# A two-block hybrid layer in fp32: index keys joined with head weights, scores dealt out between products, a split moved among selection rounds, and an output in token halves

## What is computed

```python
h = rms_norm(x, norm_g) * (1 + scale) + shift
ssm_u, ssm_z, q, k, v, attn_z, q_idx, k_idx, w_idx = split(h @ w_in)   # k_idx 64 wide, w_idx 8
z = gelu(s5(ssm_u)); z = z * sigmoid(z @ w_glu + b_glu)                # y_ssm = z * silu(ssm_z)
rel = einsum('bqhd,bsd->bqhs', q_idx, k_idx)                           # 8 heads
score = einsum('bqh,bqhs->bqs', w_idx * 8 ** -0.5, relu(rel))          # causal
_, sel = top_k(score, 128)
...
merged = sum(gates * projected)                                        # three branches
x = x + rmsnorm(merged @ w_out2, norm_mix_post)
h = rmsnorm(x, norm_ffn_pre)
x = x + rmsnorm((silu(h @ w_gate) * (h @ w_up)) @ w_down, norm_ffn_post)
```

## Time and profile before

| | |
|---|---|
| median of 3 runs | 1620.63 us (1618.85 to 1621.23) |
| the profiled execution's own time | 1621.4 us |
| its span, first to last instruction | 1619.6 us |
| mean granted TensorE clock | 0.972 of 2.4 GHz |
| PE busy | 1520.5 us (94%) |
| DVE busy | 884.5 us (55%) |
| ACT busy | 592.2 us (37%) |
| DMA | 152.24 MB, mean 94 GB/s |

### The profile page before, as it was taken

The page is one execution under the profiler, slowest core; times in us unless marked ns, Lnnn a source line. Parts: engine busy times, 40 slices in busy tenths (PEclk is TensorE's granted clock), DMA queues, the critical chain, the costliest instruction groups (busy, mean ns, idle before and its releaser), DMA issues.

```text
span 1619.6 us, 19347 instructions
## 1 busy us (share of the span) xinstructions
PE 1520.5 (94%) x7862; PEld 1209.2 (75%) x7862; DVE 884.5 (55%) x1383; ACT 592.2 (37%) x875; POOL 23.7 (1%) x36
## 2 busy tenths in 40 slices
PE   4899994989999999999999999999998999999995
PEld 2576783666888788777788887888876888888884
DVE  6878858687554766243635534553347644444233
ACT  3333423466333655133425533332334322222220
POOL 0010110000000000000000000000000000000000
PEclk9898997999999999999999999999998999999998
DMA  8422152204322121121222221222331323222221
GB/s 324 158 90 69 67 127 95 78 27 156 130 104 79 53 78 54 52 79 59 98 89 101 79 79 52 79 88 95 104 130 52 105 104 104 91 92 98 98 91 52
DMA packets 23271, 152.24 MB, mean 94 GB/s; under 512 B 3328, under 2 KB 3888, under 8 KB 6912
## 3 DMA queue, kind: packets, MB, share of 16 engines
q1 hardware_dynamic: 20720, 137.43, 24.0%
q0 software_dynamic: 2464, 13.59, 3.0%
HBM read 144.55 MB, written 7.88 MB: 94 GB/s over the span
## 4 chain that ended last, share of the span: by engine, by line
PE 87%; DVE 8%; ACT 2%; issue 1%; DMA 1%; SPq 0%; DVEq 0%; ACTq 0%
PE bank L530 85%; DVE score L1992 1%; DVE small L1991 1%; DMA xr<-xT 1%; PE bank L936 1%; DVE rstd L1784 1%; DVE w_lo L1764 0%; ACT w_hi L1154 0%; DVE sgb L1728 0%; DVE down L2579 0%; DVE tval L1950 0%; DVE y_lo L1779 0%; PE bank L868 0%; DVE score L2021 0%; DVE h_lo L1779 0%
## 5 line engine op out<-in xcount | busy, mean ns | idle before, releaser
L530 PE MATMUL bank<-h_hi,w_hi 128*128 128x512 f32 x1112 | 446.5, 402 | 12.0 <-DVE h_lo L2516 7.8
L530 PE MATMUL bank<-h_hi,w_lo 128*128 128x512 f32 x1128 | 443.6, 393 | 0.0
L530 PE MATMUL bank<-h_lo,w_hi 128*128 128x512 f32 x1112 | 437.3, 393 | 0.0
L1764 DVE TENSOR_TENSOR w_lo<-w_raw,w_hi 128x2048 fp32r<-128x2048 f32 (+2 forms) x109 | 245.5, 2253 | 269.4 <-ACT w_hi L1154 267.6
L1154 ACT CAST w_hi<-w_raw 128x2048 fp32r<-128x2048 f32 (+2 forms) x110 | 206.3, 1875 | 178.1 <-PE bank L530 175.5
L530 PEld LDWEIGHTS bank<-h_hi,w_hi 128*128 128x128 f32 x1112 | 210.8, 190 | 67.8 <-issue 21.0
L530 PEld LDWEIGHTS bank<-h_hi,w_lo 128*128 128x128 f32 x1128 | 213.5, 189 | 46.4
L530 PEld LDWEIGHTS bank<-h_lo,w_hi 128*128 128x128 f32 x1112 | 210.9, 190 | 45.0 <-issue 1.7
L530 PE MATMUL bank<-y_hi,w_hi 128*128 128x512 f32 x272 | 112.7, 414 | 22.1 <-DVE y_lo L1779 22.1
L530 PE MATMUL bank<-y_hi,w_lo 128*128 128x512 f32 x272 | 106.9, 393 | 0.0
L530 PE MATMUL bank<-y_lo,w_hi 128*128 128x512 f32 x272 | 106.7, 392 | 0.0
(11 more groups left out here) (365 smaller groups left out, 1830.8 us busy)
## 6 DMA issues: line engine op xcount, KB each, us to landing
w_raw<-wstream SPq DMA_DIRECT2D x120, 1024.0 KB, 4.8
xr<-xT SPq DMA_DIRECT2D x2, 2048.0 KB, 10.2
w_raw<-wstream SPq DMA_DIRECT2D x4, 768.0 KB, 4.2
bias_rows<-bias_table POOLq DMA_DIRECT2D x1, 2560.0 KB, 13.0
bias<-bias_rows POOLq DMA_DIRECT2D x1, 2048.0 KB, 12.4
x_saved<-xr POOLq DMA_DIRECT2D x1, 2048.0 KB, 9.6
xr<-x_saved POOLq DMA_DIRECT2D x1, 2048.0 KB, 9.0
outT<-down SPq DMA_DIRECT2D x8, 256.0 KB, 2.0
```

The costliest lines, as they stand in the source:

```text
L530: return pe.matmul(out, lhsT, rhs, start=start, stop=stop)
L1764: dve.tensor_tensor(w_low_of(s)[:, 0:kt, :], w_raw[:, i % RAW_SLOTS, 0:kt, :], hi_of(s)[:, 0:kt, :].bitcast(f32), ALU.subtract).then_inc(w ...
```

## The change

Five edits come together. (1) The tile of the index keys holds 64 key columns and 8 head-weight columns side by side, one product makes 72 rows, ACT copies the keys and scales the head weights, and a POOL DMA copies the keys to the other 64 partitions. (2) Two relevance matmuls stand after every second step of the q products, a fourth bank is used, and DVE's rotations, low splits and two selection rounds are cut into pieces with one piece behind a score. (3) `toep` is cleared by ACT. (4) 14 of the 23 selection rounds stand ahead of the low split of the first glu tile, 9 behind. Six of the low parts of `merged` are made before the last two merge steps. (5) The last group of `ffn_down` runs over all three tiles for tokens 0 to 255 and then for 256 to 511, the third tile has its high part in `w_wide`, and statistics, root, reciprocal, last operations and DMAs are done for each half. Names of semaphores and some plain renamings are left out.

```diff
-    ("k_idx", [("w_in", 0, KT, [(3584, 64), (3584, 64), (3648, 8)])]),
+    ("k_idx", [("w_in", 0, KT, [(3584, 64), (3648, 8)])]),
...
+        WIDE = (G["ffn_up"][1].s, G["ffn_down"][3].s + 2)
+        HALF = SEQ // 2
         def hi_of(s):
-            return w_wide[:, :, :] if s == G["ffn_up"][1].s else w_hi[:, s % 2]
+            return w_wide[:, :, :] if s in WIDE else w_hi[:, s % 2]
...
+        REL_BANKS = (5, 6, 7, 3)
+        ROTATE = {8: (1, 0), 9: (1, 1), 10: (1, 2), 11: (2, 0), 12: (2, 1), 13: (2, 2), 14: (3, 0), 15: (3, 1),
+                  16: (3, 2), 17: (4, 0), 18: (4, 1), 19: (4, 2), 24: (5, 0), 25: (5, 1)}
...
+            pool.wait_ge(ki_copied, 1)
+            pool.dma_start(ki[64:128, :], ki[0:64, :]).then_inc(ki_doubled, 16)
...
-            pool.memset(toep[:, :, :], 0.0).then_inc(toep_zero, 1)
...
-                mm(bank[b[0]][:, :], wh[:, k, 0:P], h_hi[:, k, :], k == 0, False)
-                mm(bank[b[0]][:, :], wh[:, k, 0:P], h_lo[:, k, :], False, False)
-                ins = mm(bank[b[0]][:, :], wl[:, k, 0:P], h_hi[:, k, :], False, k == KT - 1)
-            ins.then_inc(group_done, 1)
-            for k in range(KT):
-                out = bank[b[1]][0:HEADS, :]
-                mm(out, wh[:, k, P:P + HEADS], h_hi[:, k, :], k == 0, False)
-                mm(out, wh[:, k, P:P + HEADS], h_lo[:, k, :], False, False)
-                ins = mm(out, wl[:, k, P:P + HEADS], h_hi[:, k, :], False, k == KT - 1)
-            ins.then_inc(group_done, 1)
+                out = bank[b[0]][0:64 + HEADS, :]
+                mm(out, wh[:, k, 0:64 + HEADS], h_hi[:, k, :], k == 0, False)
+                mm(out, wh[:, k, 0:64 + HEADS], h_lo[:, k, :], False, False)
+                ins = mm(out, wl[:, k, 0:64 + HEADS], h_hi[:, k, :], False, k == KT - 1)
+            ins.then_inc(group_done, 2)
...
-                    if i >= 3:
-                        pe.wait_ge(relu_ready, i - 2)
-                    mm(bank[5 + i % 3][:, 0:P * (qt + 1)], qi[hp, h // 2, qt * P:qt * P + P],
+                    if i >= 4:
+                        pe.wait_ge(relu_ready, i - 3)
+                    mm(bank[REL_BANKS[i % 4]][:, 0:P * (qt + 1)], qi[hp, h // 2, qt * P:qt * P + P],
...
+            pe.wait_ge(ki_doubled, 16)
             relevance(0, 3)
+            pe.wait_ge(wi_ready, 1)
+            relevance(3, 4)
             for w, gr in enumerate(G["q"]):
                 for half in range(2):
                     n = 2 * w + half
-                    gemm_half(gr, half, "fm", h_hi, h_lo)
-                    relevance(3 + 8 * n, min(11 + 8 * n, 32))
-                    if n:
-                        query_stats(n - 1)
+                    for k in range(KT):
+                        gemm_unit(gr, half, k, h_hi, h_lo)
+                        if k % 2:
+                            i = 8 * n + k + 3
+                            relevance(i, min(i + 2, 32))
+                        if n and k == 5:
+                            query_stats(n - 1)
...
+            for gr in G["ffn_down"][:3]:
                 gemm_long(gr, f_hi, f_lo, AT["f"])
-            presummed("post2")
-            last_stats("post2")
+            def end_stats(t):
+                c, s0 = end_cols(t), SQ0["post2"] + 6 + 2 * t
+                out = stat_bank("post2")[:, c]
+                pe.wait_ge(root_ready, ROOT["post2"] + t)
+                pe.wait_ge(presum_ready, PRESUM.index("post2") + 1)
+                mm(out, ones[:, :], rstd[:, c], True, False)
+                for half in range(2):
+                    pe.wait_ge(sq_ready, s0 + half + 1)
+                    mm(out, ones[:, :], sqb[:, half, c], False, half == 1).then_inc(sq_used, 1)
+            gr = G["ffn_down"][3]
+            for t in range(2):
+                for half in range(2):
+                    pe.wait_ge(bank_free[end_bank(t, half)], end_uses(t, half))
+                for j, kt in enumerate(gr.kts):
+                    wh, wl = hi_of(gr.s + j), w_low_of(gr.s + j)
+                    pe.wait_ge(w_low, gr.s + j + 1)
+                    for half in range(2):
+                        c = slice(half * P, half * P + P)
+                        out = bank[end_bank(t, half)][:, 0:HALF]
+                        for k in range(kt):
+                            a = KT * j + k
+                            pe.wait_ge(act_low, AT["f"] + a + 1)
+                            mm(out, wh[:, k, c], f_hi[:, a, end_cols(t)], a == 0, False)
+                            mm(out, wh[:, k, c], f_lo[:, a, end_cols(t)], False, False)
+                            ins = mm(out, wl[:, k, c], f_hi[:, a, end_cols(t)], False, a == FT - 1)
+                        if j == 2:
+                            ins.then_inc(end_done, 1)
+                        if t and j == 0 and half == 0:
+                            end_stats(0)
+            end_stats(1)
...
+            bk = pbanks(gr)
+            act.wait_ge(group_done, 2 * gr.g + 1)
+            act.copy(ki[0:64, :], bank[bk[0]][0:64, :]).then_inc(ki_copied, 1)
+            act.activation(sqb[64:64 + HEADS, 0, :], bank[bk[0]][64:64 + HEADS, :], ACT.Copy,
+                           scale=float(HEADS) ** -0.5).then_inc(wi_row, 1)
+            act.wait_ge(ki_copied, 1)
+            act.wait_ge(wi_row, 1)
+            for half in range(2):
+                act.nop().then_inc(bank_free[bk[half]], 1)
...
-            relus(0, 3)
+            relus(0, 4)
             for n in range(4):
                 if n == 2:
                     ahead(G["q"][1])
-                relus(3 + 8 * n, min(11 + 8 * n, 32))
+                relus(4 + 8 * n, min(12 + 8 * n, 32))
                 head_chunk("q", n, q32)
+            act.activation(toep[:, :, :], ones[:, 0:1, None].to_broadcast([P, GROUPS, P]), ACT.Copy, scale=0.0)\
+               .then_inc(toep_zero, 1)
...
+            for t in range(2):
+                c, s0 = end_cols(t), SQ0["post2"] + 6 + 2 * t
+                for half in range(2):
+                    act.wait_ge(end_done, 2 * t + half + 1)
+                    act.wait_ge(sq_used, s0 + half - 1)
+                    act.activation(sqb[:, half, c], bank[end_bank(t, half)][:, 0:HALF], ACT.Square).then_inc(sq_ready, 1)
+                act.wait_ge(sq_used, s0 + 2)
+                act.wait_ge(rstd_ready, ROOT["post2"] + t)
+                act.activation(root[:, c], stat_bank("post2")[:, c], ACT.Sqrt, bias=eps[:, 0:1],
+                               scale=1.0 / D).then_inc(root_ready, 1)
...
+                if i // 4 in (1, 5):
+                    split_low_part(6 + i // 16, i % 4)
+                if i in ROTATE:
+                    rotations(*ROTATE[i])
+                if i in (26, 27):
+                    select_keys(1)
...
+            select_keys(14)
             split_low(G["glu"][0].s)
-            select_keys(23)
+            select_keys(9)
...
+            def merged_low(m):
+                dve.nop().then_inc(act_val, 1)
+                low(AT["merged"] + m, h_lo[:, m, :], h_hi[:, m, :], merged[:, m, :])
             for j in range(16):
                 if j % 2 == 0:
                     ahead(G["merge1"][j // 2])
+                if j == 14:
+                    for m in range(6):
+                        merged_low(m)
                 merge_part(1, j)
-            for m in range(KT):
-                dve.nop().then_inc(act_val, 1)
-                low(AT["merged"] + m, h_lo[:, m, :], h_hi[:, m, :], merged[:, m, :])
+            merged_low(6)
+            merged_low(7)
...
+            for t in range(2):
+                c = end_cols(t)
+                dve.wait_ge(root_ready, ROOT["post2"] + t + 1)
+                dve.reciprocal(rstd[:, c], root[:, c]).then_inc(rstd_ready, 1)
+                dve.wait_ge(rstd_ready, ROOT["post2"] + t + 1)
+                dve.wait_ge(end_done, 2 * t + 2)
+                for m in range(KT):
+                    src = down[:, m, c] if m < 6 else bank[end_bank(t, m - 6)][:, 0:HALF]
+                    stt(sgb[:, m % 2, c], src, v("norm_ffn_post", m), rstd[:, c], ALU.mult, ALU.mult)
+                    dve.tensor_tensor(down[:, m, c], xr[:, m, c], sgb[:, m % 2, c], ALU.add).then_inc(out_ready, 1)
```

More of the change, by code:

```diff
@@ L362, in uses, with end_bank, end_uses, end_cols @@
             return sum(1 for j in range(i) if bank_of(j) == bank_of(i))
+        WIDE = (G["ffn_up"][1].s, G["ffn_down"][3].s + 2)
+        HALF = SEQ // 2
         def hi_of(s):
-            return w_wide[:, :, :] if s == G["ffn_up"][1].s else w_hi[:, s % 2]
+            return w_wide[:, :, :] if s in WIDE else w_hi[:, s % 2]
+        def end_bank(t, half):
+            return bank_of(2 * G["ffn_down"][3].g + 2 * t + half)
+        def end_uses(t, half):
+            i = 2 * G["ffn_down"][3].g + 2 * t + half
+            return sum(1 for j in range(i) if bank_of(j) == bank_of(i))
+        def end_cols(t):
+            return slice(t * HALF, t * HALF + HALF)
         def w_low_of(sl):
@@ L1151, in split_high @@
```

(50 more changed lines are left out.)

35 lines of the change are left out of this document (10 added, 25 removed).

## The result

The changed kernel takes 1583.3 us, median of 4 runs (1582.1 to 1584.5), against 1619.8 us on the same chip: ratio 0.9774, interval 0.9762 to 0.9786. The gain is 36.5 us of medians. The profiled execution took 1583.07 us with a span of 1581.3.

What follows compares the result with a forecast made beforehand. PE was taken as the chain nearly everywhere, with time to gain at its waits, removable work and low clock. Terms 1.25 + 5.1 + 17.8 + 4.6 + 4.0 = 32.75 us off 1621.4 gave 1588.6, forecast 1588 us, range 1582 to 1597.

Steps and rivals of the forecast that it cites:

- Index keys: Keys and head weights in one product: q_idx starts 2.9 us earlier, less 1.65 of clock; 1.25 us gained, between 0 and 2.9.
- The clock charge: At q_idx: PE's stop of 2.5 us lets the clock fall, charged at 1.65 us against the 2.9 gained.
- Scores: First relevance matmul to first k product: 44.7 us for 51.5, 6.8 less, minus 1.7 of low clock; 5.1 us gained.
- Toep: Clearing moved from POOL to ACT, ahead of the last query root: 3.8 us under 4.2 of cover, cost 0.
- Glu: Low split between selection rounds: PE stands 3 us instead of 20.6; 17.6 gained, perhaps 0.4 of clock, 17.8 taken.
- Low parts of merged: Six made before the last merge steps: PE's stop there goes, 2.95 plus 1.65 us of clock, 4.6 gained.
- Token halves: Last down product and its tail: tail 6.6 us shorter, less 3.5, plus 0.9 for overlap and DMA; 4.0 us gained.
- Rival (a): Score stage stays near 50 us, each score waiting for a ReLU behind head copies; 1593 us; 15%.
- Rival (b): Glu split: something other than the rounds holds z or glu back, 10 of 17.8 us gained; 1596 us; 8%.
- Rival (c): No low clock in the first two parts (index keys, scores): gains of 2.9 and 6.8 us, 1585 us; 12%.
- Rival (d): Last product: weight loads show at 256 columns, 132 x 0.194 = 25.6 us more, 1614 us; 2%.
- Rival (e): Clock stays at 1.2 GHz all through the score stage, +31 us, so the kernel is slower: 1625 us; 1%.

Runs made afterwards that it cites:

- the kernel with 16 rounds: Changed kernel with the two selection rounds of the score stage moved behind it, 16 instead of 14 ahead of the glu split: 1580.6 us against 1583.3.
- glu alone: Kernel before with only 14 of the 23 selection rounds put ahead of the low split of the first glu tile: 1602.0 us against 1620.0, ratio 0.989.
- bunched orders: Changed kernel with relevance products, score steps, rotations, splits, selection rounds and banks as before: 1591.4 us; the kernel before and the one with only the glu edit are also bunched.
- the late low parts: Changed kernel with the low parts of merged put back behind the last merge step: 1592.6 us (1590.5 to 1594.5).
- the fourth round before attention: Changed kernel with four things more, among them a fourth selection round in the glu products and the cut at token 320: 1581.2 us.

## Why the prediction was right

The time came out at 1583.3 us for 1588 forecast; 36.5 us gained for 32.75 summed. Of the steps:

- **Index keys** (1.25 forecast). The 2.9 us less and the stop of 2.5 us are as worked out. The clock charge of 1.65 us was right as a likely event and wrong for the trace that came first: it applies in seven of nine. Undone: 1.7 us. The reason given for it was too strong: the prediction says that the clock fell after every stop of over 1.7 us that it read, but the trace of before has one of 2.10 us at 348.8, which it didn't read, with full clock behind it.
- **Scores** (6.8 less 1.7). The stage is 45.3 us for 44.7 forecast, and DVE's pace bounds it, as the kernel with 16 rounds shows (2.0 us less for 1.84 us of rounds taken out). The half clock behind the stop, 1.7 us forecast, came too: 1.35 us in the first trace (95.75 against 94.4), 1.6 in the second (94.36 against the 92.75 of glu alone, which has the same half clock near 220 and none behind the stop). Against bunched orders the stage is 6.2 to 7.5 us shorter. What I took for a detail, the fourth bank, may matter: the one trace of the changed order without it is 5.6 us longer there, most of it half clock, a link that the prediction lacked; the medians say 2.1, within the noise, so its usual worth is open.
- **Toep** (0). Right, both ways: ACT needs 3.6 us, under the k product, and back on POOL costs nothing.
- **Glu** (17.8: 17.6, and some of a possible 0.4 of clock). 17.5 in the trace and 18.0 alone. The split had 3.27 us to spare, for the 2.9 worked out. The 0.4 us of clock did not come: glu starts at half clock as before, for about as long (16.56 us to the logits before, 16.97 and 16.46 now).
- **Low parts of merged** (2.95 and 1.65). 2.96 and 1.71, and 1.2 us more behind the next stop. This term was too small because I looked for the clock only behind the stop that goes.
- **Token halves** (4.0). 4.4. The products take 33.1 us (1535.26 to 1568.34) for 29.9: +3.2 for 3.5 forecast. The tail goes from 18.1 to 10.7 us: 7.4 for the 7.5 forecast with the overlap. The other 0.2 us are behind the last DVE operation (2.4 to 2.2 us).

The traces sum to 38.3 us for the first (of which 2.6 is the clock between attention and merge) and to 35.1 for the second, with the same program. The second, piece by piece: 1.0 us up to the first relevance matmul (1.25 forecast), 6.3 in the scores and the piece behind them (5.1), 17.5 at glu (17.8), 0.2 in attention and up to the merge (nothing), 5.7 for the low parts of merged (4.6), 4.4 at the end (4.0). In the 6.3 there is luck of 1.6 us: the half clock behind the stop is paid, and as much is given back near 220 us, where this execution has 3.4 us of it for the 6.8 of before. The missing 3.7 us of my sum are therefore in part the 1.1 us behind `merged`, 0.4 at the end and 1.2 in the scores; what is left is within the 2 to 5 us by which the changed kernel's executions differ.

Rival (a) fell: DVE waits 1.1 us in the score stage, once. Rival (b) fell with the glu kernel. Rival (c) took place in half: no low clock at q_idx in the first trace. Rival (d) fell for 256 columns, yet there is a floor of 0.112 us a matmul, met at 192 and 128 columns, that looks like its mechanism. The Trainium skill (TensorE: Matmul & The Clock Gate, Part 2, LDWEIGHTS (loading the stationary operand)) puts a load at its columns over 1.2, 107 ns for 128; the 0.112 us here agree. The sentence of Part 3 of that page by which a load overlaps a running matmul only when the row group differs doesn't: at 0.120 us with 256 columns and 0.2267 with 512, the loads on the same 128 rows are hidden. Rival (e) fell: 0.99 of full clock over the stage.

What stays open: why the half clock follows the stop before 322 us in some executions and those before 274 and 479 in others, and in two of fourteen the short one before 836; what the fourth bank is worth as a rule; and 3.5 us of the late low parts.

## What to carry to other kernels

Cut both traces at the same instructions and compare the pieces: it separates an edit's few microseconds from those that the clock moves elsewhere, which here are as large, in one and the same program. Fill an idle stretch of the helper engine with work taken from where that engine sets the pace; but look at what follows the new place, as the fourth round before attention showed. Count a stop on PE with the half clock behind it, as likely and not as certain (seven of nine stops of 2.3 to 2.5 us had it at q_idx), and look behind the next stop too. When tokens are cut, stop at the width where a matmul no longer gets cheaper, here between 192 and 256 columns.

## What was not expected of the hardware

- A matmul on 128 by 128 weights takes 0.120 us with 256 columns, 0.147 with 320 and 0.2267 with 512, but 0.112 with 192, 128 and 64.
- The granted clock fell to 0.50 for a few microseconds behind stops of PE, but behind different ones in two executions of one program, which were 2.5 us apart in a piece of 868 us. Twice it fell 2 us behind a stop of 0.86 us, while the stop of 2.3 us before attention had no half clock behind it in six of fourteen traces.
- The order with three banks had stops of the same sum as with four (3.9 and 3.8 us), but over 13 us at 0.50 in the stage in its one trace.
- A DVE operation of 128 columns took 4,096 ns beside a POOL memset that touches neither of its tensors, and 226 ns beside the same clearing on ACT.
